# Second mixer of a two-layer decoder step: state products dealt out between value projections and numerator products

## The reference

```python
z = h @ P['cd_w_in'][o]
qc, kc, vc, gc, qkd, vd, ig, fg, og = split_cols(z, [...])
...
# retention, per head
scores = jnp.einsum('bjhd,bshd->bhjs', q, k) * dmask[None]
intra = jnp.einsum('bhjs,bshe->bjhe', scores, v)
inter = jnp.einsum('bjhd,bhde->bjhe', q, S) * jnp.exp((j[:, None] + 1.0) * lg[None, :])[None, :, :, None]
...
# mLSTM, per head
num = jnp.einsum('bjsh,bshe->bjhe', A, v) + sc[..., None] * jnp.einsum('bjhd,bhed->bjhe', q, C)
den = jnp.sum(A, axis=2) + sc * jnp.einsum('bjhd,bhd->bjh', q, n)
h = num / jnp.maximum(jnp.abs(den), jnp.exp(-m_j))[..., None]
```

## Time and profile before

| | us |
|---|---|
| median of three timed runs | 1473.85 (1472.66 to 1474.93) |
| profiled execution, its own time | 1469.65 |
| span of the profiled execution, first to last instruction | 1467.9 |
| PE busy in the span | 1400.2 (95%) |
| DVE busy in the span | 1071.5 (73%) |
| mean granted TensorE clock | 0.974 |

### The profile page before, as it was taken

The page is one execution under the profiler, slowest core; times in us unless marked ns, Lnnn a source line. Parts: engine busy times, 40 slices in busy tenths (PEclk is TensorE's granted clock), DMA queues, the critical chain, the costliest instruction groups (busy, mean ns, idle before and its releaser), DMA issues.

```text
span 1467.9 us, 28300 instructions
## 1 busy us (share of the span) xinstructions
PE 1400.2 (95%) x11458; PEld 1285.4 (88%) x11458; DVE 1071.5 (73%) x1381; ACT 350.0 (24%) x664; POOL 361.9 (25%) x304
## 2 busy tenths in 40 slices
PE   6999999999878998999999999999999999999997
PEld 6999999996333787999999999999996669999997
DVE  7987686767976746697769597768568576887664
ACT  3111102003345333521110221110202454211110
POOL 2533112000540022543321253321200002533310
PEclk9999999999997999999999999999999879999998
DMA  8443452664877203544336344345161315444142
GB/s 308 154 171 114 175 177 89 211 224 146 270 281 255 96 4 146 211 159 171 143 136 218 134 171 153 133 153 199 73 224 59 142 40 210 156 172 171 49 162 88
DMA packets 62698, 233.14 MB, mean 159 GB/s; under 512 B 9003, under 2 KB 18544, under 8 KB 45580
## 3 DMA queue, kind: packets, MB, share of 16 engines
q1 hardware_dynamic: 50426, 224.56, 42.9%
q10 hardware_dynamic: 11554, 6.37, 1.4%
q0 software_dynamic: 624, 0.87, 0.2%
HBM read 225.54 MB, written 6.10 MB: 158 GB/s over the span
## 4 chain that ended last, share of the span: by engine, by line
PE 50%; DVE 4%; POOL 3%; ACT 1%; issue 1%; DMA 0%; POOLq 0%; DVEq 0%; ACTq 0%
PE psum L191 15%; PE psum L193 15%; PE psum L192 15%; DVE x L410 1%; DVE hidden_hi L406 1%; DVE rstd L312 1%; POOL hidden L320 0%; DMA ring<-in_w_cd 0%; POOL hidden L322 0%; DVE x_lo_r L306 0%; POOL ysq_ab_out L2968 0%; PE psum L366 0%; PE psum L363 0%; PE psum L2762 0%; POOL sq_cd_out L320 0%
## 5 line engine op out<-in xcount | busy, mean ns | idle before, releaser
L191 PE MATMUL psum<-x_hi_r,pair_hi 128*128 128x288 f32 x1736 | 515.7, 297 | 6.3 <-DVE up L615 2.7
L193 PE MATMUL psum<-x_hi_r,ring_r 128*128 128x288 f32 x1736 | 514.6, 296 | 0.0
L192 PE MATMUL psum<-x_lo_r,pair_hi 128*128 128x288 f32 x1608 | 474.8, 295 | 0.0
L186 DVE TENSOR_TENSOR ring_r<-ring,pair_hi 128x2048 fp32r<-128x2048 f32 (+1 forms) x127 | 338.4, 2666 | 21.7 <-ACT pair_hi L181 17.8
L191 PEld LDWEIGHTS psum<-x_hi_r,pair_hi 128*128 128x128 f32 x1736 | 328.2, 189 | 9.1 <-issue 7.6
L193 PEld LDWEIGHTS psum<-x_hi_r,ring_r 128*128 128x128 f32 x1736 | 327.7, 189 | 0.0
L192 PEld LDWEIGHTS psum<-x_lo_r,pair_hi 128*128 128x128 f32 x1608 | 303.4, 189 | 0.3
L191 PE MATMUL psum<-hidden_hi_r,down_hi 128*128 128x288 f32 x704 | 208.4, 296 | 0.0
L192 PE MATMUL psum<-hidden_r,down_hi 128*128 128x288 f32 x704 | 207.7, 295 | 0.0
L193 PE MATMUL psum<-hidden_hi_r,down_r 128*128 128x288 f32 x704 | 207.0, 294 | 0.0
L673 POOL TENSOR_TENSOR hidden<-silu,up 128x288 f32 x88 | 126.5, 1437 | 123.0 <-ACT silu L599 121.3
(11 more groups left out here) (547 smaller groups left out, 1869.1 us busy)
## 6 DMA issues: line engine op xcount, KB each, us to landing
ring<-in_w_gu SPq DMA_DIRECT2D x88, 1024.0 KB, 4.8
down<-in_w_down SPq DMA_DIRECT2D x64, 704.0 KB, 4.4
ring<-in_w_ab SPq DMA_DIRECT2D x18, 1024.0 KB, 5.3
ring<-in_w_cd SPq DMA_DIRECT2D x12, 1024.0 KB, 6.1
ring<-in_cache_k SPq DMA_DIRECT2D x32, 256.0 KB, 4.9
index_keys<-in_cache_k SPq DMA_DIRECT2D x32, 256.0 KB, 4.9
index_keys<-in_cache_i ACTq DMA_DIRECT2D x64, 64.0 KB, 2.8
eight_pages_ds<-in_cache_v SPq DMA_DIRECT2D x16, 256.0 KB, 5.2
```

Source lines behind the costliest of these rows:

```text
L186: return eng.tensor_tensor(lo, a, hi.bitcast(F32), ALU.subtract)
L191: pe.matmul(out, w_hi, x_hi, start=start, stop=False)
L192: pe.matmul(out, w_hi, x_lo, start=False, stop=False)
L193: return pe.matmul(out, w_lo, x_hi, start=False, stop=stop)
```

## The change

On TensorE, row groups 1 and 2 of mLSTM's values are no longer projected in one run ahead of the retention outputs. Row group 1 + hp is projected among the state products of head pair hp: one k step (three matmuls), then the state products of one sequence for two heads, eight times. The waits for the decayed queries and for rs0 now stand ahead of these row groups.

In the numerators the 32-row product of a side moves up behind its 256-column product, and the 128-column product of a side goes behind the spreads, each followed by the state products of two sequences.

On ScalarE the silus stand ahead of the copy of the last value rows and of the copies of the retention outputs.

```diff
-            for i in range(3):
-                value_rows(1, i)
-            for h in range(4):
-                act.wait_ge(S["y_sum"], h + 1)
-                act.activation(hN[:, h], B[h][:, 0:NT], ACT.Copy).then_inc(S["y_out"], 1)
+            value_rows(1, 0)
+            value_rows(1, 1)
             act.wait_ge(S["conv_done"], 1)
             for a in range(4):
                 act.activation(qk[:, a], cacc[:, a], ACT.Silu).then_inc(S["silu_done"], 1)
             for h in range(4):
                 act.activation(ymix[:, h], GC[:, h], ACT.Silu).then_inc(S["gates_done"], 1)
+            value_rows(1, 2)
+            for h in range(4):
+                act.wait_ge(S["y_sum"], h + 1)
+                act.activation(hN[:, h], B[h][:, 0:NT], ACT.Copy).then_inc(S["y_out"], 1)
...
-            def values(w, tiles):
-                project_values(c, pe, first + (VC, VD)[w], lambda i, mm: mm.then_inc(*((v_sum, 1) if i < 2 else (c.pair_done, 2))), tiles)
+            def values(w, tiles, ks=range(KT)):
+                project_values(c, pe, first + (VC, VD)[w], lambda i, mm: mm.then_inc(*((v_sum, 1) if i < 2 else (c.pair_done, 2))), tiles, ks)
...
             values(1, (0,))
-
-            values(1, (1, 2))
...
                 for b in range(NB):
                     o = TP + b * TS
+                    values(1, (1 + hp,), range(b, b + 1))
                     for h in two:
                         mm = pe.matmul(B[h][:, o:o + TS], rs0[half(h % 2), b, hp], qdec[half(h % 2), hp, b * TS:b * TS + TS], start=False, stop=True, **sg_)
...
                     pe.matmul(B[bn][:, 0:TP], l0, scT[:, 4 + h, 0:TP], start=True, stop=False, **sg_)
-                    pe.matmul(B[bn][:, P:TP], l1, scT[:, 4 + h, TP:ST_COLS], start=False, stop=True, **sg_)
+                    pe.matmul(B[bn][:, TP:NT], l2, scs[:, 4 + h], start=False, stop=False, **sg_)
                 if hp == 0:
                     for h in (2, 3):
                         pe.wait_ge(S["var_used"], h - 1)
                         spread(h, 6 + h % 2)
-                for h, bn, l0, l1, l2 in sides:
-                    pe.matmul(B[bn][:, TP:NT], l2, scs[:, 4 + h], start=False, stop=False, **sg_)
-                for b in range(NB):
-                    o = TP + b * TS
-                    for h in two:
-                        pe.matmul(B[2 * h][:, o:o + TS], c0t[half(h % 2), b, hp], qsc[half(h % 2), hp, b * TS:b * TS + TS], start=False, stop=True, **sg_)
+                for i, (h, bn, l0, l1, l2) in enumerate(sides):
+                    pe.matmul(B[bn][:, P:TP], l1, scT[:, 4 + h, TP:ST_COLS], start=False, stop=True, **sg_)
+                    for b in (2 * i, 2 * i + 1):
+                        o = TP + b * TS
+                        for g in two:
+                            pe.matmul(B[2 * g][:, o:o + TS], c0t[half(g % 2), b, hp], qsc[half(g % 2), hp, b * TS:b * TS + TS], start=False, stop=True, **sg_)
```

## The result

The changed kernel is slower by 0.9%, by about what was forecast (12.5 us).

A forecast was written before the change was run, and what follows sets the result against it. TensorE, busy 95%, bounds most of the span, but waits decide in the changed stretch. Chain 8.3 + first numerators 1.2 + second 3.0 = 12.5 us, on 1473.85 makes 1486.4 us; own range 1481 to 1490.5.

The forecast's parts named there:

- trips: TensorE: each way from full-row products to products on fewer rows and back costs 0.27 us.
- A value group, 1.20: Dealt value rows: three value products, then four state records, take 1.20 us a group; last value product 11.5 us later.
- Rival 1: Value groups: alternation nearly free at 0.93 us, memset costs 4.1, numerators about 0; 1478 us, chance 0.15.
- VectorE's chain, 8.3: Memset, VB, output-pair split, L2439: the 11.5 us delay less 3.25 slack makes 8.3 us (4.1 to 9.8).
- The clock among the groups: Dealt value groups on TensorE: 1.20 us a group at full clock, as most of each group is dense.
- Rival 2: Dealt value groups: clock falls to half in one third of the value rows, 6.5 us more; 1493 us, chance 0.15.
- Rival 3: 1142 through 1204 us: dealing holds the clock full; 1470.4 us, chance 0.05 whole, 0.10 for its half without change.
- First numerators, 1.2: First head pair: seven more trips cost 1.9 us, 0.72 hidden by TensorE's wait for var_used, so 1.2 shows.
- Second numerators, 3.0: Second head pair: nothing hides the trips; extra 1.9 to 5.9 us depending on the clock, taken as 3.0.
- Everything behind has nothing to lose: Behind the numerators (L2813 to L2816): already at half clock, so no further loss.
- Edits at nothing: Earlier rs0 wait, earlier silus on ScalarE, and SyncE's later c0t, c0 and output-pair transfers: no cost or gain.

The follow-up runs named there:

- second comparison: Changed kernel unchanged, timed in more rounds against the kernel before: 1483.34 against 1470.76 us, ratio 1.0092 (1.0057 to 1.0127).
- double groups: Changed kernel with value rows dealt in twos, six value products then the states of two sequences: 1483.05 against 1469.61 us of before, ratio 1.0095.
- The kernels that relieve VectorE alone: Changed kernel, VectorE reordered: output-pair split ahead of the memset wait, 1478.69 us, 1.0076 to before; VB also behind weighed keys, 1477.80, 1.0055.

## Why the prediction came out right

The sum was 12.5; the medians say 13.2 and 12.6, the ratios 14.3 and 13.5. The way there was the forecast's: late memset, late L2439, trips and half clock in the numerators. That the total of 1486.4 was met to 0.1 us (1486.42) is luck: it is a median of 4 executions between 1479.9 and 1491.28, the second comparison gave 1483.34, and the medians of before differ by 6 us from one comparison to the next. Point by point:

- **A value group, 1.20.** Measured 1.21 to 1.23 on 128 rows and 1.12 on 32. The forecast took both alike, and they aren't: with 128 columns of weights the first value product of a group takes 0.33 to 0.35 to the next (1129.99 to 1130.34; 0.23 in a dense row), with 32 only 0.25 (1141.77 to 1142.02). So the memset came 11.2 later and not 11.5. The double groups show the same price by another way. Rival 1 (alternation free, 0.93) is out.
- **VectorE's chain, 8.3.** Measured 7.86: 11.20 less the slack of 3.25 is 7.95. The kernels that relieve VectorE alone show that it is this chain. The forecast said that TensorE would be idle some 6 us and it was 7.53. That step forgot that the second exponent row waits for L2450 to L2452 too, 2.2 us behind the start of L2439; it carried no term of the sum.
- **The clock among the groups.** It was full for all of the 28.6 us from 1122.4 to 1151.0, where before it fell at 1142.88. Rival 2 is out. Rival 3 was right on this place and wrong on the rest: the gain fell into a stretch in which TensorE waits, and the clock was half in the second numerators. The Trainium skill, "TensorE: Matmul & The Clock Gate", section "Why this matters for your kernels", speaks of idle gaps; the half clock of 1154.3 to 1164.5, with 4.08 busy of 10.20, agrees, that of 1195.2 to 1208.8, with 13.60 busy of 13.60, isn't explained by it.
- **First numerators, 1.2.** Measured 1.20 (8.81 against 7.61, 0.72 of it idle). The work grew by 8.81 - 6.89 = 1.92, seven trips of 0.27, as forecast.
- **Second numerators, 3.0.** Measured 4.16. This is the term that was mis-sized, by 1.2. The step took the value "nearer to the stretch where the clock did return"; once it had fallen within the pair it returned in neither profile ahead of the first mean. Its first two pieces ran at full clock and all else at half. An estimate from these rows: with the clock full the pair would take 8.81 less the two spreads in the first one (1188.06 to 1189.13, 1.07), 7.7; so 4.6 of 12.38 are the clock's. In before, by the same count, 8.22 less (6.89 - 1.07) is 2.4. Of the 4.16, then, 1.9 are trips and 2.2 more half clock.
- **Everything behind has nothing to lose.** In the second profile it is so up to the fourth mean: 9.34 from the first, as before. In the first profile 2.4 came back there, since the clock was full from 1208.8, and in both about 1.1 behind it. The step left out that there was something to win: at the end of the span the two profiles are 10.1 and 12.3 later, not 13.2.
- **Edits at nothing.** No idle time stands before the first state product, so the earlier wait for rs0 cost nothing. The silus stand at 1141.5 to 1144.3, the last value rows at 1150.61; alone the move changed nothing that can be told. The numerators, which read c0t and c0, began without a wait (no idle time before 1184.31).

ScalarE's order, the transfers and the wait for rs0 had no share in the result that the rows or the times show. The errors (0.4 too much for the chain, 1.2 too little for the second pair, 1 to 3 that came back behind it and stood at nothing) partly cancel. That the sum came as near as it did is in part luck.

## What to carry to other kernels

Before work is dealt out on the busiest engine, look for who waits for the last piece of each run: here a memset of 1.8 us hung on the last value product, and delaying that product by 11.2 us cost 7.9 at once, whatever the clock gained. Price the alternation from a place in the same trace where the two shapes already alternate, and multiply. And a clock that is held full is worth something only where the engine isn't about to wait: here it was full for all of 28.6 us, and TensorE then waited 7.53.

## What was not expected of the hardware

The granted clock fell in the midst of dense work. With eight 256-column products put in front of the second numerators, TensorE had been busy without a gap, and the clock fell to 1.2 GHz 0.66 us into them, 3.4 us long; the engine had come from the first pair's 128-column and 4-column products at full clock. The last of the added products and the mixed ones that followed then ran at 2.4 GHz for 6.8 us, and the clock fell again. What decides the moment wasn't found.

The half-clock stretches also moved by more than the work did, and from one execution to the next of the same kernel. The version with groups of two had 6.8 us of them ahead of the numerators where the changed kernel had 3.4, and that ate the rest of a 2.2 us gain. But that can't be put down to its order: the changed kernel's own two profiles have 10.2 and 6.8 us of half clock in the wait for VectorE, and 13.7 and 20.5 from the second numerators on, and the kernel with the numerators alone was 4.5 us late ahead of its first edited product. A profile of one execution tells an order of work safely, but a sum of a few us only up to where its clock differs from another execution's.
